# First stage of a diffusion block kernel: all modulation slabs on TensorE in 32-column tiles, decay factors on ScalarE

## The reference, cut to what matters

```python
mod = silu(c) @ mod_w[layer] + mod_b            # shift, scale, gate, ... (6 x 2048)
h = modulate(rms_norm(x, g), shift, scale)      # then the projections of the layer
# filters: hid is 256 positions x 64, made by a small sine MLP
h = (hid @ w3).reshape(n_tok, 2, D)
h = h * exp(-offs[:, None, None] * deltas)      # decay window
h = h * rsqrt(sum(h * h, axis=0) + EPS)
```

## Time and profile before

| what | us |
|---|---|
| median of three executions | 2601.32 |
| lowest, highest | 2597.08, 2603.92 |
| span of the profiled execution | 2601.3 |
| time of the execution that agrees with it | 2601.32 |
| TensorE matmul busy, share | 2461.9, 95% |
| TensorE weight load busy, share | 2070.6, 80% |
| VectorE busy, share | 1951.6, 75% |
| ScalarE busy, share | 1170.5, 45% |
| mean granted TensorE clock | 0.971 |

### The profile page before, as it was taken

The page is one execution under the profiler, slowest core; times in us unless marked ns, Lnnn a source line. Parts: engine busy times, 40 slices in busy tenths (PEclk is TensorE's granted clock), DMA queues, the critical chain, the costliest instruction groups (busy, mean ns, idle before and its releaser), DMA issues.

```text
span 2601.3 us, 39595 instructions
## 1 busy us (share of the span) xinstructions
PE 2461.9 (95%) x13332; PEld 2070.6 (80%) x13332; DVE 1951.6 (75%) x2352; ACT 1170.5 (45%) x1611; POOL 0.2 (0%) x4
## 2 busy tenths in 40 slices
PE   6879998888999999999998999999899999999998
PEld 2248876777788888888887888888778888888887
DVE  6767777688988877877888889878786565555665
ACT  2235256535444444444446444434534444444444
POOL 0000000000000000000000000000000000000000
PEclk9989998898999999999998999999899999999999
DMA  8856865476988888888786655647696665665653
GB/s 311 299 205 229 290 189 180 150 272 236 323 307 276 289 283 281 278 273 278 270 273 236 235 197 194 235 162 239 213 341 212 189 187 187 188 190 185 188 189 124
DMA packets 441211, 610.37 MB, mean 235 GB/s; under 512 B 18875, under 2 KB 383644, under 8 KB 439068
## 3 DMA queue, kind: packets, MB, share of 16 engines
q1 hardware_dynamic: 439676, 599.98, 69.3%
q10 hardware_dynamic: 1440, 9.18, 1.0%
HBM read 596.50 MB, written 10.49 MB: 233 GB/s over the span
## 4 chain that ended last, share of the span: by engine, by line
PE 75%; DVE 9%; ACT 6%; issue 5%; DMA 5%; SPq 1%; DVEq 0%; ACTq 0%
PE ps L371 43%; PE ps L380 22%; DMA raw<-in_mlp_w 3%; PE ps L1139 2%; DVE w_lo L456 2%; PE ps L1371 2%; DVE acc L468 2%; ACT w_hi L452 2%; ACT hm L900 1%; PE ps L1361 1%; DVE sm L1803 1%; DMA raw<-in_attn_w_out 1%; PE ps L1156 1%; PE ps L442 1%; PE ps L1175 1%
## 5 line engine op out<-in xcount | busy, mean ns | idle before, releaser
L452 ACT ACTIVATE w_hi<-raw 128x1024 fp32r<-128x1024 f32 x720 | 761.5, 1060 | 1088.1 <-PE ps L380 857.9
L456 DVE TENSOR_TENSOR w_lo<-raw,w_hi 128x1024 fp32r<-128x1024 f32 x720 | 877.8, 1223 | 465.6 <-ACT w_hi L452 462.0
L371 PE MATMUL ps<-lat,w_hi 128*128 128x512 f32 x3136 | 817.3, 400 | 35.8 <-ACT w_hi L452 16.4
L371 PEld LDWEIGHTS ps<-lat,w_hi 128*128 128x128 f32 x3136 | 572.3, 191 | 148.4 <-issue 33.4
L371 PE MATMUL ps<-alt,w_hi 128*128 128x512 f32 x2624 | 675.0, 396 | 10.4 <-DVE alt L1790 6.2
L371 PEld LDWEIGHTS ps<-alt,w_hi 128*128 128x128 f32 x2624 | 476.0, 190 | 97.5 <-issue 6.6
L380 PEld LDWEIGHTS ps<-lat,w_lo 128*128 128x128 f32 x3136 | 433.7, 191 | 31.8 <-DVE w_lo L456 0.4
L380 PE MATMUL ps<-lat,w_lo 128*128 128x256 f32 x3136 | 446.1, 283 | 0.0
L380 PEld LDWEIGHTS ps<-alt,w_lo 128*128 128x128 f32 x2624 | 362.6, 191 | 28.4 <-DVE w_lo L456 2.7
L468 DVE SCALAR_TENSOR_TENSOR acc<-slab,silu,acc 128x1024 f32<-128x1024 f32 x300 | 378.6, 1279 | 8.0 <-DMA slab<-in_mod_w 7.0
L380 PE MATMUL ps<-alt,w_lo 128*128 128x256 f32 x2624 | 373.7, 283 | 1.9 <-DVE w_lo L456 1.9
(11 more groups left out here) (191 smaller groups left out, 1495.5 us busy)
## 6 DMA issues: line engine op xcount, KB each, us to landing
raw<-in_mlp_w SPq DMA_DIRECT2D x512, 512.0 KB, 3.8
slab<-in_mod_w SPq DMA_DIRECT2D x352, 512.0 KB, 6.0
raw<-in_hy_w_in SPq DMA_DIRECT2D x96, 512.0 KB, 4.4
raw<-in_attn_w_in SPq DMA_DIRECT2D x48, 512.0 KB, 4.6
raw<-in_mod_w SPq DMA_DIRECT2D x32, 512.0 KB, 6.9
raw<-in_attn_w_out SPq DMA_DIRECT2D x32, 512.0 KB, 4.6
raw<-in_hy_w_out SPq DMA_DIRECT2D x32, 512.0 KB, 5.8
spec_dram<-spec ACTq DMA_DIRECT2D x8, 1024.0 KB, 7.3
```

The source lines that it names most:

```text
L371: e.matmul(ps[:, bank, :], w_hi[:, n % RING, kk, fb * P:(fb + 1) * P], t[:, kb, :], start=(kb == 0), stop=False)
L452: e.activation(w_hi[:, n % RING], raw[:, n % RING], ACT.Copy).then_inc(hi_ready, 1)
L456: e.tensor_tensor(w_lo[:, n % RING], raw[:, n % RING], w_hi[:, n % RING].bitcast(F32), ALU.subtract).then_inc(split_ready, 1)
```

## The change

In constants, the table `decay` goes; `deltas` (128x512 a quarter, equal rows) and in `const` two columns `pick` (ones at partitions 0, 32, 64, 96 for c and at 1, 33, 65, 97 for c_ctx) and two of negative offsets come. All `Fori` loops of the stage are written out. The core of the diff:

```diff
 # SP
-  for j in range(16): ... slab j; at j == 1: w3 and decay of this quarter; at j in (4, 7): x, ctx of this quarter
+            for c in range(4):
+                for j in range(16):
+                    e.wait_ge(start_free[j % START_RING], 2 * c + j // START_RING + 1)
+                    e.dma_start(start_slot(j), a["mod_w"][...]).then_inc(start_landed[j % START_RING], 16)
+                    if c == 0 and j == 1:
+                        sp_taps(0)            # w3 and deltas (256 KB each)
+                    if c < 3 and j == 11:
+                        sp_taps(c + 1)
+                    if j in (3, 6, 9) and j // 3 - 1 < len(TOK_LOADS[c]):
+                        ...                   # parts of x, ctx: TOK_LOADS = ((0, 1, 2), (3, 4, 5), (6, 7), ())
 # TensorE
+            def pe_slabs(c, g):
+                if c > 0 and g == 0:
+                    e.wait_ge(rows_copied, c)
+                for j in (2 * g, 2 * g + 1):
+                    e.wait_ge(start_landed[j % START_RING], 16 * (2 * c + j // START_RING + 1))
+                for b in range(2):
+                    for j in (2 * g, 2 * g + 1):
+                        t = 32 * (j % 4)
+                        mm = e.matmul(ps[t:t + 32, 4 + b, :], pairs[:, j], start_slot(j)[:, b * 512:(b + 1) * 512],
+                                      start=(j < 4), stop=(j >= 12))
+                        if b == 1:
+                            mm.then_inc(start_free[j % START_RING], 1)
+            def pe_close_start(c):
+                e.wait_ge(rows_copied, c + 1)
+                e.wait_ge(spec_copied, 4 * (2 * c + 1) + 3 + 1)
+                for b in range(half):
+                    mm = e.matmul(ps[:, 7, 2 * b:2 * b + 2], rows[:, c % 2, b * P:(b + 1) * P], pick,
+                                  start=True, stop=True)
+                mm.then_inc(start_turned, 1)
+            for c in range(4):
+                pe_taps(c, 0)
+                pe_slabs(c, 0)
+                if c > 0:
+                    pe_close_start(c - 1)
+                pe_slabs(c, 1)
+                if c < 3:
+                    pe_slabs(c, 2)
+                pe_spectrum(c, 0)
+                pe_slabs(c, 3 if c < 3 else 2)
+                pe_taps(c, 1)
+                if c < 3:
+                    pe_slabs(c, 4)
+                pe_slabs(c, 5 if c < 3 else 3)
+                pe_spectrum(c, 1)
+                if c < 3:
+                    pe_slabs(c, 6)
+                    pe_slabs(c, 7)
+            pe_slabs(3, 4)
+            e.wait_ge(taps_ready, 2 * 3 + 1 + 5)
             e.wait_ge(sq_summed, 10)
             ...                               # the 16 sums of squares
+            pe_slabs(3, 5)
+            e.wait_ge(spec_copied, 4 * 7 + 3 + 1)
             pe_spread(e, 0, 4)
+            pe_slabs(3, 6)
+            pe_slabs(3, 7)
+            pe_close_start(3)
             pe_iter(e, T_Q0, lat, lambda j: (norm_ready, 2 * j + 1, 2 * j + 2))
 # ScalarE
+            def make_decay(c):
+                e.wait_ge(in_deltas[c % 2], 16 * (c // 2 + 1))
+                e.wait_ge(taps_ready, 2 * c + 2)
+                for tb in range(2):
+                    ins = e.activation(decay[:, c % 2, tb], deltas[:, c % 2], ACT.Exp,
+                                       scale=const[:, OFFS + tb:OFFS + tb + 1])
+                ins.then_inc(decay_made, 1)
+            make_decay(0)                     # ahead of quarter 0; make_decay(c + 1) at the end of quarter c
+                if c == 3:
+                    act_root(e, 0, 4)
+                e.wait_ge(start_free[(2 * 7 + 1) % START_RING], 2 * c + 3)
+                e.activation(rows[:, c % 2].rearrange("p (b n) -> p b n", b=2), ps[:, 4:6, :], ACT.Copy).then_inc(rows_copied, 1)
-            act_split(e, T_Q0, 0)
-            act_split(e, T_Q0, 1)
             for p in range(8):
                 act_norm_hi(e, *NORM_X, p)
-                if p in (1, 3):
-                    act_split(e, T_Q0, p // 2 + 2)
+                if p in START_SPLITS:         # (0, 1, 3, 5)
+                    act_split(e, T_Q0, START_SPLITS.index(p))
 # VectorE
+            e.memset(pairs[:], 0.0).then_inc(silu_v, 1)
+            e.tensor_scalar(pairs[:, :, 0:2], silu[:].rearrange("p (w k) -> p k w", w=2), 1.0, None,
+                            ALU.mult).then_inc(pairs_ready, 1)
-  both passes over VectorE's slabs, the sums over transposed blocks (mod_part), start_part
+            def start_close(c):
+                e.wait_ge(start_turned, c + 1)
+                for w, dst in enumerate((mod, mod_ctx)):
+                    ins = e.tensor_tensor(dst[:, half * c:half * (c + 1)], ps[:, 7, w:2 * half:2],
+                                          vec("mod_b", half * c, half), ALU.add)
+                ins.then_inc(start_summed, 1)
+            for c in range(4):
+                start_taps(c, 0)              # the three operations on the taps, as before
+                if c > 0:
+                    start_close(c - 1)
+                for i in TOK_LOADS[c]:
+                    ...                       # sum of squares of part i
+                start_taps(c, 1)
             ...                               # reciprocal root
+            for p in range(4):
+                dve_normalise(e, *NORM_X, p)
+            start_close(3)
             dve_gain(e, 1, gain[:, 0:KB], mods(0, 1), vec("mix_g", 0, KB))
             dve_gain(e, 2, gain[:, KB:2 * KB], mod_ctx[:, KB:2 * KB], vec("mix_g", 0, KB))
+            for p in range(8):
                 dve_norm_lo(e, *NORM_X, p)
+                if p in START_SPLITS:
+                    dve_split(e, T_Q0, START_SPLITS.index(p))
+                if p < 4:
+                    dve_normalise(e, *NORM_X, p + 4)
```

More of the change, by code:

```diff
@@ L103, in constants @@
     mask = np.stack([np.where(k + P - q <= WINDOW, 0.0, -1e30), np.where(q + P - k <= WINDOW, 0.0, -1e30)], 1)
-    const = np.concatenate([ident, swap], 1)
+    pick = np.stack([np.arange(P) % 32 == w for w in range(2)], 1).astype(f32)
     rope = np.concatenate([np.cos(ang), np.sin(ang) * sign, mask.reshape(P, 2 * P)], 1)
@@ L222, in vec @@
             return vecs[:, ds(VECS[name] + i, n)]
-        in_const, in_vecs, in_x, in_ctx = sem("in_const"), sem("in_vecs"), sem("in_x"), sem("in_ctx")
+        in_const, in_vecs = sem("in_const"), sem("in_vecs")
+        in_tok = [sem(f"in_tok{i}") for i in range(8)]
         in_fw, in_feats, in_fwd0 = sem("in_fw"), sem("in_feats"), sem("in_fwd0")
@@ L343, in sp_values @@
                     sp_slabs(e, sl, 1, (n - 4) * 4, 4)
+        START_SPLITS = (0, 1, 3, 5)
+        TOK_LOADS = ((0, 1, 2), (3, 4, 5), (6, 7), ())
         def start_slot(j):
@@ L1001, in _ @@
             e.dma_start(fwd0[:], a["fwd"]).then_inc(in_fwd0, 16)
-            e.wait_ge(started, 1)
[L1005 to L1022, removed]
@@ new lines, in pe_taps, with pe_spectrum @@
+            def pe_taps(c, o):
+                if o == 0:
+                    e.wait_ge(in_w3[c % 2], 16 * (c // 2 + 1))
+                e.wait_ge(taps_ready, 2 * c + o + 4)
+                for tb in range(2):
+                    mm = e.matmul(ps[:, tb, :], hid_2[:, tb * P:(tb + 1) * P], w3[:, c % 2, o, :],
+                                  start=True, stop=True)
+                mm.then_inc(taps_mm, 1)
+            def pe_spectrum(c, o):
+                e.wait_ge(taps_ready, 2 * c + o + 5)
+                e.wait_ge(spec_copied, 4 * (2 * c + o) + 2)
+                if o == 0:
+                    e.wait_ge(start_summed, c + 1)
+                for b in range(4):
+                    for tb in range(2):
+                        e.transpose(ps[:, 6 + b // 2, (b % 2) * TOK + tb * P:(b % 2) * TOK + (tb + 1) * P],
+                                    taps[:, o, tb, b * P:(b + 1) * P], ident)
+                for f in range(4):
+                    e.wait_ge(spec_copied, 4 * (2 * c + o) + f + 1)
+                    e.matmul(ps[:, 2 + f % 2, :], fwd0[:, f * P:(f + 1) * P], taps[:, o, SIDE[f], :],
+                             start=True, stop=True).then_inc(spec_mm, 1)
@@ L1438, in _ @@
                     if o == 0:
[L1440 to L1446 removed]
+                        for i in TOK_LOADS[c]:
+                            e.wait_ge(sq_summed, i + 1)
+                            e.wait_ge(in_tok[i], 16)
+                            e.activation(sq[:, i % 2], (x, xc)[i // 4][:, 4 * (i % 4):4 * (i % 4) + 4, :],
+                                         ACT.Square).then_inc(squares, 1)
@@ new lines, in start_close @@
+            def start_close(c):
[4 more added lines that the diff above has]
+                ins.then_inc(start_summed, 1)
+            for c in range(4):
+                start_taps(c, 0)
+                if c > 0:
+                    start_close(c - 1)
+                for i in TOK_LOADS[c]:
+                    e.wait_ge(squares, i + 1)
+                    at = TOK * (i // 4)
```

(3 more changed lines are left out.)

163 lines of the change are left out of this document (43 added, 120 removed).

## The result

| what | before | after |
|---|---|---|
| median of four executions each, us | 2602.53 | 2569.62 |
| lowest, highest, us | 2597.08, 2603.92 | 2569.16, 2570.96 |
| span of the profiled execution, us | 2601.3 | 2568.2 |
| mean granted TensorE clock | 0.971 | 0.972 |

The ratio is 0.9879 with a 95% interval of 0.9865 to 0.9893: 33 us faster, and 33.1 between the two profiled spans. The prediction said 20 to 21 us and a range that holds the result. Where the time came from is plain from two starts: ScalarE begins with part 0 of x at 153.71 us instead of 186.92, 33.2 earlier, and the last part's rest is ready at 171.50 instead of 202.83, 31.3 earlier. From that rest to the end of the kernel the two profiles differ by 1.8 us more (2398.5 and 2396.7).

The account below looks back on a forecast made before the run. It took TensorE's chain of waits, with the quarter's closing, as the bound. Quarters of 33.9 us and the tail put the last part at 182.5, 20.3 us earlier: 2601.3 - 20.3 = 2581, with slack 2580; range 2562 to 2608.

Parts of the forecast that it names:

- the price of the slabs: Slab matmuls on TensorE: sixteen slabs a quarter at two records per 0.437 us, 14.0 us, plus 2.2 us for run ends.
- has idle enough: VectorE: sixteen slab passes a quarter and the closing sums go; memset and scatter, some 0.8 us, fit a wait: nothing added.
- eight slots at 5.4 us from issue to landing cover it: Slab transfers: the slots cover TensorE's longest stretch without taking a slab, 5.8 us plus taps.
- rival 3: More overlap, transfers bind: 0.44 us a slab, 134 busy us of transfers, last slab at 136, 2560 us; chance 0.07.
- (1): Sign on TensorE: slab records of two tiles start nearly together, a run of 16 records takes about 3.9 us; 7.0 without overlap.
- (2): Sign in the stage: quarters of 34 us, where they were about 41.
- (3): Sign at quarter ends: TensorE doesn't wait between last spectrum and next taps; rows are copied in the time of the taps.
- (4): Sign in the tail: first L900 activation on ScalarE at about 165 us, last part's rest 18 us behind.
- (5): Sign in the quarters: ScalarE waits for TensorE, not the reverse; DMA share near 0.95.
- The switch between tile sizes: TensorE changing matmul kind ten times a quarter instead of eight: 0.3 us a quarter; 0.3 us more per switch gives 2592.
- the 3 us of transfers: Decay loads of 512 KB become deltas of 256 KB: 1 MB less in all, 3 us at 357 GB/s.
- the one added term: ScalarE's tail: splits of units 0 and 1, 1.99 us, now among the parts, so 15.9 us becomes 17.9.

## Why the prediction was right in direction and short in size

Direction and range were right, and the mechanism (TensorE's chain binds the stage; take the closing off it, and overlap pays for eight more slabs) stands in the main, as one tile alone loses it all; after the change VectorE's order and the transfers hold TensorE up too. The forecast gain was 20.3 us and the profiled one up to the last part's rest 31.3. The 11 us, span by span:

| stretch | predicted | measured | difference |
|---|---|---|---|
| first quarter, from 13.75 | 36.5 | 34.1 | 2.4 |
| second | 33.9 | 32.5 | 1.4 |
| third | 33.9 | 33.5 | 0.4 |
| fourth, to the last slab | 42.0 | 36.0 | 6.0 |
| last slab to part 0 | 4.5 | 3.9 | 0.6 |
| part 0 to the last rest | 17.9 | 17.8 | 0.1 |

**The step that failed** is the price of the slabs: "so I take a record of the next tile to start beside the second record of the one before", 0.875 us a slab and 0.44 for each broken run. I wrote of four tiles at once as the lower end and gave it 0.07. The measured price is 1.9 us a run, with two slabs or with four in it. Five runs a quarter are 9.3 us at their best, not 16.2, and seven in the fourth 12.9, not 17.1 (from the start of one to the next instruction a run is 1.84 or 1.87). The reason I gave, that the waits in the code allow that pairing and no more, took a limit on the order of issue for a limit on what runs at once; the two records of one matmul share a place and are in series, but four tiles do not share it. The Trainium skill (TensorE: Matmul & The Clock Gate, Part 3) has three column tiles at 2.38 times one; this case's float32 runs show 1.92 times with two (6.98 to 3.63) and 3.6 with four (6.98 to 1.94).

**Why the quarters came near right nonetheless.** TensorE's own work would have made them 27 us. A second step failed against the first: I wrote that VectorE "has idle enough" and that "eight slots at 5.4 us from issue to landing cover it". VectorE does idle, but its order holds the second taps behind two or three sums, for 11.0 us in the first three quarters; and the landing time of a queue with room did not hold for a full one, 9.5 us. TensorE idled 5.3 to 5.7 us in each of these quarters: 11.0 in all for the taps, 4.5 for copies to `spec` and 0.7 for a slab. The low clock behind two of the waits for taps added 3. The full transfers are rival 3: its 134 busy us are the 134.9 of the window (0.93 x 145). Its 2560 isn't reached, because VectorE's order and the fourth quarter, where the share falls to 0.70, keep the transfers from running through; the version with longer runs in the last quarter and the second taps first measured 2561.

**The fourth quarter** held over half of the error, and that by terms, not by waits: slab runs 4.2 us too dear, the sums of squares 3.7 instead of 4.8, the spread 1.1 instead of 2.0. The these came from stand at a low clock: granted were 0.75 from 177.4 to 182.2 us and 0.50 from 182.2 to 186.1. My sum said that a full clock would give 2 back, and here it did; that was luck. In the same place with the second taps first they took 4.41 and 2.01 us, so it is the clock and not the place between slabs that makes them cheap.

**Point by point.** (1) A run of 16 records in 3.9 us: no, 1.9. (2) Quarters of 34: yes, for the reasons above, not mine. (3) No wait between the last spectrum and the next taps: right, at 45.95 to 47.81. The rows' copy is hidden; the closing's 2.4 us measured 1.95. Its place is worth more than the wait it avoids, as a slow clock followed each such wait. (4) Part 0 at about 165: 153.7; 18 to the last rest: 17.8. (5) ScalarE waits for TensorE and the share is near 0.95: right (0.96, 1.01 and 0.97), though no term of the sum held a wait for it. The switch between tile sizes, which I left at 0.16 us, showed no more: that rests on 1.91 for a run between two kinds of matmul, 4 x 0.437 + 0.16. My reason why records of the kernel before are in series, one output place, was loose: they went to two banks, and share the tile. **Decay:** nothing on ScalarE, right; the 3 us of transfers, which I left out of the sum, may count: with the table loaded the last rest came 3.1 us later, at the edge of what can be told. **Tail:** the one added term, two splits for 2.0 us, was right, but the old order would have paid as much in another place.

What stays open: how far VectorE's order and the transfers each bind, what the decay part is worth, and what makes the clock fall behind some waits and not behind others.

## What to carry to other kernels

Where a stationary operand is narrow, spread successive float32 matmuls over the four 32-column tiles, in order of the tiles: a run then costs its busiest tile, so few long runs beat many short ones. When the bound engine is relieved by a quarter, price the next two limits with it: the transfers' busy time as a sum, with landing times of a full queue, and the order of the helper engine between two things that the chain needs. Put a short dependent step behind work that doesn't need it; waits of 1.5 us ahead of sixteen narrow records cost the stage over 3 us each, twice their length. And compare kernels by the point in the trace where the changed stage ends, as 2400 us of unchanged work behind it scatter by more than a small gain.

## What the runs showed of the hardware that was not expected

- Four column tiles work at once, as if with a queue each: four slabs take 6.98, 3.63 and 1.94 us in one, two and four tiles.
- A wait of 1.52 us on TensorE, followed by sixteen matmul records of two columns (1.95 us), stood ahead of a fall of the granted clock from 1.00 to 0.50 (2.4 to 1.2 GHz) in three of three places. In the changed kernel the same sixteen records between slab runs, with no wait, had no such fall behind them in three of three. A wait is not needed for a fall: behind the 32 records of one column (3.6 to 5.0 us), with no wait beside them, the next slab run was slow in ten of eleven kernels with 32-column tiles. Nor is one enough: of the waits of 4.58, 3.55 and 2.90 us for the taps, the first and the last had a low clock behind them (0.58 and 0.72), the second 1.00.
- With 512 KB loads and 1 MB stores together the DMA engines are full (shares of 1.01 to 1.03) at 371 to 397 GB/s. A 512 KB slab lands 9.5 us behind its issue in the changed kernel, whose share up to 145 us is 0.93, against 5.4 before, at 0.83.
